# A two-layer Hyena/RG-LRU mixture-of-experts step: where the router's logits come from, and which engine modulates

## The reference, cut to what matters

```python
def rms_norm(x, g):
    y = x32 * lax.rsqrt(jnp.mean(x32 * x32, axis=-1, keepdims=True) + NORM_EPS)
    return (y * g.astype(jnp.float32)).astype(x.dtype)

x = x + g1 * m                                          # m: the mixer's output
h = rms_norm(x, p['norm_moe'][i]) * (1 + sc2) + sh2     # modulation: context and latent have their own
x = x + g2 * moe_ffn(h, p['router_w'], ...)
```

## Time and profile before

| what | value |
|---|---|
| median of 3 runs | 1588.24 us (1586.63 to 1589.04) |
| the profiled execution's own time | 1582.39 us |
| its span, first to last instruction | 1580.6 us |
| mean granted TensorE clock | 0.978 of 2.4 GHz |
| PE busy | 1473.4 us (93% of the span) |
| DVE busy | 631.9 us (40%) |
| ACT busy | 297.4 us (19%) |
| DMA | 495.29 MB, mean 313 GB/s |

### The profile page before, as it was taken

One profiled execution on the slowest core, in us unless ns is written; L12 is line 12 of the kernel. 1 busy time (PEld: TensorE's weight loads), 2 busy tenths in 40 slices (PEclk: granted clock), 3 DMA queues, 4 the chain that ended last, 5 costly groups with the idle time before them and its releaser, 6 DMA issues.

```text
span 1580.6 us, 21260 instructions
## 1 busy us (share of the span) xinstructions
PE 1473.4 (93%) x7790; PEld 712.1 (45%) x7791; DVE 631.9 (40%) x1845; ACT 297.4 (19%) x503; POOL 0.2 (0%) x4
## 2 busy tenths in 40 slices
PE   6999999997799999989999799997989999999996
PEld 3454555654244344344344355554344444344433
DVE  4445665333314322322333448745122333432333
ACT  4322222131010011010010247623010011011001
POOL 0000000000000000000000000000000000000000
PEclk9999999998999999999999899998999999999999
DMA  9538667762969999999996601435899999999992
GB/s 326 197 134 297 254 255 262 297 281 94 392 264 397 427 427 426 425 427 428 424 414 241 237 1 54 201 118 213 339 399 427 424 429 423 401 428 428 424 402 97
DMA packets 67711, 495.29 MB, mean 313 GB/s; under 512 B 4608, under 2 KB 21264, under 8 KB 28368
## 3 DMA queue, kind: packets, MB, share of 16 engines
q1 hardware_dynamic: 66048, 489.33, 76.0%
q10 hardware_dynamic: 1616, 5.33, 1.1%
HBM read 493.06 MB, written 1.58 MB: 313 GB/s over the span
## 4 chain that ended last, share of the span: by engine, by line
PE 77%; DMA 11%; DVE 6%; ACT 3%; issue 2%; ACTq 0%; DVEq 0%; SPq 0%
PE PS L846 75%; DMA halves<-in_moe_w 11%; PE PS L850 2%; DVE xc L1853 1%; ACT hT L580 0%; DVE misc L1671 0%; DVE halves L1671 0%; DVE halves L1662 0%; DVE halves L1664 0%; ACT hT L829 0%; DVE halves L1490 0%; DVE halves L1663 0%; ACT halves L640 0%; ACT halves L742 0%; ACT h L641 0%
## 5 line engine op out<-in xcount | busy, mean ns | idle before, releaser
L846 PE MATMUL PS<-halves,hT 128*64 128x512 f32 x3072 | 673.0, 597 | 15.2 <-DMA halves<-in_moe_w 12.6
L846 PEld LDWEIGHTS PS<-halves,hT 128*64 128x64 f32 x3072 | 218.1, 138 | 452.0 <-issue 430.4
L846 PE MATMUL PS<-hT,halves 128*128 128x384 f32 x640 | 216.4, 494 | 1.9 <-ACT hT L580 1.9
L846 PE MATMUL PS<-halves 128*32 128x512 f32 (+5 forms) x928 | 194.1, 509 | 1.8 <-ACT halves L543 0.7
L846 PEld LDWEIGHTS PS<-hT,halves 128*128 128x128 f32 x640 | 120.8, 192 | 99.1 <-issue 21.1
L1934 DVE COPY misc<-PS 64x512 f32<-64x512 f32 x32 | 21.9, 683 | 333.7 <-PE PS L846 333.7
L846 PEld LDWEIGHTS PS<-halves 128*128 128x128 f32 (+2 forms) x928 | 96.6, 158 | 85.2 <-issue 44.5
L1853 DVE SCALAR_TENSOR_TENSOR xc<-PS,MOD,xc 128x128 f32<-128x128 f32 x336 | 112.3, 409 | 13.8 <-PE PS L846 11.8
L846 PE MATMUL PS<-stack,h 128*128 128x128 f32 x768 | 98.4, 288 | 18.9 <-issue 9.9
L846 PEld LDWEIGHTS PS<-stack,h 128*128 128x128 f32 x768 | 94.0, 202 | 30.5 <-issue 26.3
L602 ACT ACTIVATE hT<-PS 128x512 f32<-128x512 f32 x32 | 19.1, 597 | 430.7 <-PE PS L846 430.7
(11 more groups left out here) (234 smaller groups left out, 972.2 us busy)
## 6 DMA issues: line engine op xcount, KB each, us to landing
halves<-in_moe_w SPq DMA_DIRECT2D x192, 2048.0 KB, 17.7
halves<-in_ada_w SPq DMA_DIRECT2D x48, 1024.0 KB, 6.5
halves<-in_hy_w_in SPq DMA_DIRECT2D x12, 1024.0 KB, 5.1
halves<-in_rg_w_in SPq DMA_DIRECT2D x4, 2048.0 KB, 19.1
halves<-in_hy_w_out SPq DMA_DIRECT2D x4, 1024.0 KB, 9.4
halves<-in_rg_w_out SPq DMA_DIRECT2D x2, 2048.0 KB, 9.6
halves<-in_rg_wa SPq DMA_DIRECT2D x1, 2048.0 KB, 8.3
halves<-in_rg_wx SPq DMA_DIRECT2D x1, 2048.0 KB, 10.9
```

The costliest lines, as they stand in the source:

```text
L846: return nc.tensor.matmul(out, lhsT, rhs, start=start, stop=stop)
```

## The change

The weights of the router are scaled by A once per stream (`rw_mod`, DVE, in `residual`). PE multiplies them with the residual `xc` itself (`router_raw`), between the norm's sums and the spread of the inverse roots, and B with the plain weights (`bias_mm`, two columns). ACT copies both out, loads the table of Exp, and then modulates all 8 tiles of tags 1 and 3, four before the routing's Exp and four after; DVE modulates nothing there. DVE multiplies the raw logits by the inverse roots, and its 8 products of the norm stand around the logits' maximum (6 before, 2 after). PE adds the four parts, the bias and turns the result in one go, with a constant matrix `fold` (six matmuls of 16 columns into bank 6). The token tiles come in the order of `TOKEN_ORDER`, all behind the logits. Cut to its core:

```diff
 PE:
             def norm(tag):
                 norm_sums(tag)
+                if tag % 2:
+                    router_raw(tag // 2)
                 norm_spread(tag)
-            def router(l):
-                pe.wait_ge(S("rw_in"), 16)
+            def router_raw(l):
+                pe.wait_ge(S("rw_mod"), l + 1)
                 for kk in range(2):
                     for j in range(4):
-                        channel_ready(2 * l + 1, j + 4 * kk)
-                        last = mm(PS[32 * j:32 * j + 32, 0, 0:N], rw[:, j + 4 * kk, :], hT3[:, j + 4 * kk, :],
+                        last = mm(PS[32 * j:32 * j + 32, 4, 0:2], rw[:, j + 4 * kk, :], MOD[:, l, 8 * SH2 + j + 4 * kk, :],
                                   kk == 0, kk == 1)
-                last.then_inc(S("rt_mm"), 1)
-                token_tile(l, 0)
+                last.then_inc(S("bias_mm"), 1)
+                for s, cs in streams:
+                    for kk in range(2):
+                        for j in range(4):
+                            last = mm(PS[32 * j:32 * j + 32, 5, cs], rw_mod[:, s, j + 4 * kk, :], xc[:, j + 4 * kk, cs],
+                                      kk == 0, kk == 1)
+                last.then_inc(S("raw_mm"), 1)
+
+            def router(l):
+                pe.wait_ge(S("bias_ev"), l + 1)
                 pe.wait_ge(S("rt_ev"), before("rt_ev", l) + 1)
                 for t in range(NT):
-                    last = tr(PS[:, 1, P * t:P * t + P], pre[:, 0, P * t:P * t + P])
+                    s = 0 if t == 0 else 1
+                    out = PS[:, 6, NE * t:NE * t + NE]
+                    mm(out, bias_col[:, s:s + 1].broadcast_to([P, P]), const("fold"), True, False)
+                    last = mm(out, pre[:, 0, P * t:P * t + P], const("fold"), False, True)
                 last.then_inc(S("rt_mm"), 1)
-                for i in range(1, 6):
+                for n, i in enumerate(TOKEN_ORDER):
+                    if n in (0, 3):
+                        pe.wait_ge(S("hT_act"), turned_act(2 * l + 1) + 4 * (i % 2) + 4)
+                    if 2 + i == 6:
+                        pe.wait_ge(S("rt_max"), before("rt_max", l) + 1)
                     token_tile(l, i)
 ACT:
                 norm_root(tag)
-                modulate(tag)
+                if tag % 2 == 0:
+                    modulate(tag, range(BY_ACT))
...
+                act.wait_ge(S("bias_mm"), l + 1)
+                a.activation(bias_col, PS[:, 4, 0:2], ACT.Copy).then_inc(S("bias_ev"), 1)
+                act.wait_ge(S("raw_mm"), l + 1)
+                a.activation(pre[:, 0, :], PS[:, 5, 0:N], ACT.Copy).then_inc(S("raw_ev"), 1)
                 table(ACT.Exp)
-                act.wait_ge(S("rt_mm"), before("rt_mm", l) + 1)
-                a.activation(pre[:, 0, :], PS[:, 0, 0:N], ACT.Copy).then_inc(S("rt_ev"), 1)
-                token_tile(0)
+                modulate(2 * l + 1, range(4))
                 act.wait_ge(S("rt_max"), before("rt_max", l) + 1)
                 a.activation(rt(0), rt(0), ACT.Exp).then_inc(S("rt_exp"), 1)
-                for i in range(1, 6):
-                    token_tile(i)
+                modulate(2 * l + 1, range(4, KD))
+                for n in range(6):
+                    token_tile(n)
 DVE, residual:
                 link(ins)
+                dve.wait_ge(S("modA"), 2 * l + 2)
+                dve.wait_ge(S("rw_in"), 16)
+                for s in range(2):
+                    ins = v.tensor_tensor(rw_mod[:, s, :, :], rw[:, :, :],
+                                          MODA[:, 2 * l + 1, :, s:s + 1].broadcast_to([P, KD, 32]), ALU.mult)
+                ins.then_inc(S("rw_mod"), 1)
                 for dc in range(KD):
                     dve.wait_ge(S("o_mm"), 8 * l + dc + 1)
 DVE, route (norm(2 * l + 1) ahead of it is gone):
-                link(v.memset(chosen[:, 3 * NE:], 0.0))
-                dve.wait_ge(S("rt_mm"), before("rt_mm", l) + 2)
-                parts = PS[:, 1, 0:N].rearrange("p (t j e) -> p t e j", t=NT, j=4)[:, :, 0:NE, :]
-                link(v.tensor_reduce(L, parts, AX, ALU.add))
-                link(v.tensor_reduce(mx, L, AX, ALU.max))
-                v.tensor_tensor(L, L, wide(mx), ALU.subtract).then_inc(S("rt_max"), 1)
+                tag = 2 * l + 1
+                v.memset(chosen[:, 3 * NE:], 0.0)
+                norm_inverse(tag)
+                dve.wait_ge(S("raw_ev"), l + 1)
+                dve.wait_ge(S("rb_mm"), tag + 1)
+                v.tensor_tensor(pre[:, 0, :], pre[:, 0, :], PS[:, 1, 0:N], ALU.mult).then_inc(S("rt_ev"), 1)
+                norm_apply(tag, range(6))
+                dve.wait_ge(S("rt_mm"), before("rt_mm", l) + 1)
+                logits = PS[:, 6, 0:NT * NE].rearrange("p (t e) -> p t e", t=NT)
+                link(v.tensor_reduce(mx, logits, AX, ALU.max))
+                v.tensor_tensor(L, logits, wide(mx), ALU.subtract).then_inc(S("rt_max"), 1)
+                norm_apply(tag, range(6, KD))
                 dve.wait_ge(S("rt_exp"), before("rt_exp", l) + 1)
...
+TOKEN_ORDER = (0, 2, 4, 1, 3, 5)
```

More of the change, by code:

```diff
@@ L34 @@
 NX = (N - BASE) // EXTRA
-_COLS = [("ident", P), ("earlier_rows", P // 2), ("all_rows", P // 2), ("ones", 32), ("iota_base", BASE), ("iota_extra", EXTRA), ("limits", NX), ("desc", NE)]
+_COLS = [("ident", P), ("earlier_rows", P // 2), ("all_rows", P // 2), ("ones", 32), ("iota_base", BASE), ("iota_extra", EXTRA), ("limits", NX), ("desc", NE), ("fold", NE)]
 _HYENA_COLS = [("fwd_lat", 2 * LAT), ("fwd_ctx", CTX), ("inv_lat", 4 * LAT // 2), ("inv_ctx", CTX)]
@@ L88, in constants @@
     put("iota_extra", np.tile(np.arange(EXTRA), (P, 1)))
+    put("fold", np.tile(np.eye(32)[:, 0:NE], (4, 1)))
     put("desc", np.tile(NE - np.arange(NE), (P, 1)))
@@ L144, in before, with by_act, turned_act, turned_dve @@
     return PER[name] * index
+def by_act(tag):
+    return KD if tag % 2 else BY_ACT
+def turned_act(tag):
+    return sum(by_act(u) for u in range(tag))
+def turned_dve(tag):
+    return KD * tag - turned_act(tag)
 MOE_RELEASE = ("w13_last", "w13_last", "w13_last", "w13_last", "w2_first", "w2_mm")
@@ L576, in modulate @@
                 act.wait_ge(S("modA"), tag + 1)
-                for k in range(BY_ACT):
+                for k in ks:
                     act.wait_ge(S("nrm"), before("nrm", tag) + k + 1)
@@ L681, in mixer0 @@
                 spectrum(1)
-                modulate(0)
+                modulate(0, range(BY_ACT))
                 for ct in range(24):
@@ L976, in channel_ready @@
                 if k < BY_ACT:
[L977 removed]
+                    pe.wait_ge(S("hT_act"), turned_act(tag) + k + 1)
                 else:
[L979 removed]
+                    pe.wait_ge(S("hT_dve"), turned_dve(tag) + k - BY_ACT + 1)
             def norm_ready(tag):
[L982 to L983 removed]
+                pe.wait_ge(S("hT_act"), turned_act(tag + 1))
+                pe.wait_ge(S("hT_dve"), turned_dve(tag + 1))
             def norm(tag):
                 norm_sums(tag)
+                if tag % 2:
+                    router_raw(tag // 2)
                 norm_spread(tag)
@@ L1421, in norm_inverse, with norm_apply @@
                 v.reciprocal(rs, rs).then_inc(S("rinv"), 1)
-            def norm_apply(tag):
+            def norm_apply(tag, ks):
                 if tag % 2 == 0 and tag:
@@ L1426, in norm_apply @@
                 dve.wait_ge(S("rb_mm"), tag + 1)
-                for k in range(KD):
+                for k in ks:
                     v.tensor_tensor(hT3[:, k, :], xc[:, k, :], PS[:, 1, 0:N], ALU.mult).then_inc(S("nrm"), 1)
             def modulate(tag):
-                l = tag // 2
-                sh = SH2 if tag % 2 else SH1
+                l, sh = tag // 2, SH1
                 dve.wait_ge(S("modA"), tag + 1)
@@ L1442, in norm @@
                 norm_inverse(tag)
-                norm_apply(tag)
+                norm_apply(tag, range(KD))
                 modulate(tag)
@@ L1557, in mixer0 @@
                 halves_joined(0)
-                norm_apply(0)
+                norm_apply(0, range(KD))
                 filter_norm(0)
@@ L1809, in route @@
                 link(v.tensor_tensor(gates[:, :, 0:NE], scores, wide(sm), ALU.mult))
-                dve.wait_ge(S("rt_mm"), before("rt_mm", l) + 3)
+                dve.wait_ge(S("rt_mm"), before("rt_mm", l) + 2)
                 ranks = PS[:, 1, 0:NT * NE].rearrange("p (t e) -> p t e", t=NT)
@@ L1945, in _ @@
                 residual(l)
-                norm(2 * l + 1)
                 route(l)
```

13 lines of the change are left out of this document (8 added, 5 removed).

## The result

The changed kernel takes 1569.43 us (median of 4, 1565.29 to 1574.03) against 1587.43 us (median of 4): ratio 0.9897, 95% interval 0.9877 to 0.9917. It was timed twice more, beside the experiments: 0.9907 (0.9873 to 0.9941) and 0.9900 (0.9875 to 0.9925). So about 1%, or 15 to 16 us, went; the prediction said 7.2 us, and 1576.2 at the lowest. Its profiled execution took 1570.13 us (span 1568.3), 12.3 less than that of before.

What follows compares the result with a forecast made beforehand. It took the routing's path (DVE products, ACT modulation, ACT table, PE, DVE) as the limit before the gather. Gains of 3.50 in layer 0 and 3.67 in layer 1, together 7.2 us, take 1588.24 to 1581.0; range 1576.2 to 1584.4.

Steps and rivals of the forecast that it cites:

- The raw block: PE ahead of the spread: 1.33 us of raw matmuls plus 0.40 of bias, so the spread starts 0.42 us later.
- ACT and DVE legs: Before Exp: ACT modulates 4 tiles in 3.59 us; DVE's products and maximum beside it are just hidden, by 0.14 us.
- PE's fold: Six PE matmuls beside the modulation, 1.7 us, hidden with 1.1 us of cover; about 0.5 us cost at the lower clock.
- The table load "has left the path": ACT's 1.41 us load of the Exp table now lies beside spread and products, leaving ACT free at 347.4.
- Evictions: Six ACT evictions of token tiles before the gather end at 358.3, needed at 361.1: 2.8 us of cover.
- the scaled weights: Two DVE products in `residual`, at most 0.95 us per layer, expected to cost nothing because DVE stands idle there.
- The clock of the gathers: Rival: shorter PE idle before the gathers keeps the clock up, up to 4.6 us more gain, 1576.4; chance 14%.
- late by the table: Rival: ACT or DVE starts late, as with a doubled table switch, 1.0 us per layer; gain 5.2, 1583.0; chance 14%.
- raw matmuls one after another: Rival: the raw block ahead of the spread takes 7.5 instead of 1.73 us; 4.6 us slower, 1592.8; chance 2%.
- Does a shift of the gather reach the end?: Step from gather to kernel end: weight loads wait for PE, so every us won before the gather counts once per layer.
- All that follows shifts with the gather: Claim for everything behind the gather: it moves earlier by what the routing wins, 3.50 us in layer 0, 3.67 in layer 1.

Runs made afterwards that it cites:

- b_table: Kernel before, with only ACT's load of the Exp table moved ahead of the modulation in tags 1 and 3: ratio 0.9992 (0.9976 to 1.0007).
- a_three: Kernel after, with 3 instead of 4 tiles modulated ahead of the routing's Exp, first trace: gather 16.62 and 16.61 us after the sums.
- a_three5: Kernel after, with 3 instead of 4 tiles modulated ahead of the routing's Exp, timed: ratio 0.9888 (0.9865 to 0.9912), median 1569.24 us.
- b_clean2: Kernel before, with 160 already met waits in PE's program in layer 0 only (120 before the mask, 40 behind the ranks): 1578.68 us, ratio 0.9956.
- a_raw2: Kernel after, with the 16 matmuls of the raw logits made twice: 1654.21 us (one execution).
- b_clean: Kernel before, with 200 already met waits in PE's program in layer 0 only (120 before the mask, 80 behind the ranks): 1660.04 us, ratio 1.0464.

## Why the prediction was wrong

**The direction and the mechanism of the routing were right, and its size nearly:** 7.2 forecast, 7.9 measured. Point by point:

- *The raw block* was mis-sized. I had it end 0.42 late; the spread started 0.04 late. The matmuls' own time was nearly right (raw 1.33 forecast and 1.49 measured, bias 0.40 and 0.28), but they start before the sums have ended, at 346.55 for the bias with the sums busy until 346.73, and the rows overlap: the block ends 1.43 after the sums instead of 1.73, close behind the reciprocal (1.19). The difference between 0.42 and 0.04 late, 0.38, is what layer 0 gave more than 3.50 at the small reduce (3.88). Layer 1 was 4.03 to 3.67 for the same reason.
- *ACT and DVE legs:* modulation to Exp 3.59 forecast, 350.44 to 353.96 measured. DVE waited 0.26 for Exp; 0.14 was forecast.
- *PE's fold* cost 1.5 us (350.02 to 351.5) and was covered, as said.
- *The table load "has left the path":* true, but it was no cost of its own. It lay beside PE's last logits matmuls, which my account of rows 3 passed over; b_table shows it. The sum was not hurt, since both went.
- *Evictions and the scaled weights* stayed covered; the two products took 0.76 us in layer 1, at 1049.50, where 0.95 was the bound, and DVE still stood idle 2.78 behind them.
- *The clock of the gathers* stayed a loss in all traces but two, both of the version with 3 tiles: in a_three the gather of layer 0 took 5.60 us instead of 7.1 to 8.4, and it was 22.39 us to the first extra pass, where the others take 23.9 to 25.1; in a_three5 the gather of layer 1 took 5.60. There the granted clock was still 0.50 in the last transposes (356 to 358 us in a_three), rose while PE stood idle and was 1.00 in the gather; in the kernel after it was 1.00 in the last transposes already (358 to 360) and fell to 0.50 inside the gather (365 to 367). The rival exists, and decided nothing.
- *The rivals "late by the table" and "raw matmuls one after another"* did not come: the table load and the instruction behind it took 1.28 and 0.20 and were done at 350.22, before DVE's product released the modulation at 350.44; and the 32 records took 1.49.

**The step that failed** is in "Does a shift of the gather reach the end?". "All that follows shifts with the gather" took it for granted that the expert loops cost the same after the change. They don't: the change adds 41 matmul records a layer to PE's program, each with its weight load, and that moved the borders of PE's code pieces out of the first-round gathers. It is worth 7 us here (b_clean2; 6.3 by the stretches), about as much as the routing. The sum had no term for it, and the range, built from the bounds of the routing's terms and the clock, could not hold it. The sign was visible: "issue" has 2% in the shares of the chain, and the waits of 1.73 and 3.97 us stood in that chain, but the prediction passes over them. That the change moved the code to a better place and not to a worse one was luck: nobody had counted.

**The second thing missed** is that the same term has a cliff. With 64 instructions more a layer (a_raw2, one execution) it is 68 us slower (1654.21 against 1585.93) instead of 16 us faster. No rival of mine had that size.

What stays open: in layer 1 only 3.5 of 6.0 us reach the end, for the wait for weights at 1260.60 takes the rest; which transfer would have to start sooner was not tried. The first medians lie 18.0 us apart and the profiled executions 12.3; the starts of the programs differ by up to 6 us from execution to execution, which no experiment looked into. How many pieces PE can keep was not measured, only that loops stay loaded which span 7 by my count, and not those which span 8; why the piece behind a branch's comes 5.6 to 6.2 us later is open too.

## What to carry to other kernels

Where an engine's program is long and its hot part a loop, count code as a resource: read the instruction queue's pieces on the page, look whether any are loaded while the loop goes round, and compare them when a change adds instructions ahead of it. A wait on "issue" inside a run of like matmuls in the first round may be a wait for code: look whether a piece of the instruction queue lands inside it. A few met waits in idle time can move it; time every such version, since the same edit can push the loop over what stays loaded. And when logits, statistics or any small product wait for a wide elementwise pass, look whether algebra lets them read what lies ahead of that pass: here a dependency of 11.4 us fell to 7.5 though more work was done.

## What the runs showed that I had not expected

- A loop of 1566 instructions (counted in the compiled program) runs at full speed when it touches 7 pieces of 16 KB and loses about 80 us in its rounds when it touches 8 (b_clean 1660.0 against b_clean2 1578.7, of which 2 are its late gather; a_raw2 1654.2 against 1570 for the kernel after and 2.6 for its second blocks): 95 or 96 pieces loaded instead of 31 or 32, in layer 1 (b_clean) or layer 0 (a_raw2). The Trainium skill, Runtime: NRT & Kernel Launch, section Instruction fetch mechanics, gives PE room for 2048 instructions, which is eight pieces; in these runs eight, by that count, did not stay.
- A border of a piece inside a first-round gather costs 1.7 to 4.3 us, and the clock falls behind all but the shortest: behind 3.97 us the next 13 matmuls take 3.14 us where 24 take 2.94, behind 2.10 us 22 take 4.35, behind 1.73 us 22 take 2.72. Counting PE's instructions in the trace places such a border exactly.
- 160 waits already met, 80 instructions, cost PE nothing that could be seen in 8 us of idle time; with 80 instead of 40 of them behind the ranks the gather came 2 us late (b_clean).
